# A two-layer decoder trunk: the mixing of the expert rows moves from VectorE to ScalarE and GpSimd

## The reference

```python
top_v, top_i = lax.top_k(h @ w_router, 2)
top_w = jax.nn.softmax(top_v, axis=-1)
# gates: top_w at the two experts of each token, 0 elsewhere
for e in range(N_EXPERTS):
    out = out + gates[:, e:e + 1] * ((silu(h @ w_gate[e]) * (h @ w_up[e])) @ w_down[e])
x = x + g2 * out
return rmsnorm(x, final_g)
```

## Time and profile before

| | us |
|---|---|
| median of 3 runs (lowest, highest) | 1311.26 (1309.56, 1312.83) |
| time of the profiled execution | 1308.28 |
| its span, first to last instruction | 1306.5 |
| TensorE (PE) busy | 1240.5 |
| VectorE (DVE) busy | 1082.4 |
| ScalarE (ACT) busy | 818.2 |
| GpSimd (POOL) busy | 52.3 |
| last turn, about | 1192 to 1294 |

### The profile page before, as it was taken

One profiled execution on the slowest core, in us unless ns is written; L12 is line 12 of the kernel. 1 busy time (PEld: TensorE's weight loads), 2 busy tenths in 40 slices (PEclk: granted clock), 3 DMA queues, 4 the chain that ended last, 5 costly groups with the idle time before them and its releaser, 6 DMA issues.

```text
span 1306.5 us, 17451 instructions
## 1 busy us (share of the span) xinstructions
PE 1240.5 (95%) x5431; PEld 869.8 (67%) x5431; DVE 1082.4 (83%) x1389; ACT 818.2 (63%) x1169; POOL 52.3 (4%) x71
## 2 busy tenths in 40 slices
PE   5999979999989988999999999999999999999996
PEld 1445757777767766666676676676676776776664
DVE  2858877888779766988988988998988988898896
ACT  3125534444445654777777777777777777777774
POOL 2101000000000101000000000000000000000000
PEclk8999989999999998999999999999999999999999
DMA  9996838888867435999999999999999999999991
GB/s 294 388 387 228 277 112 317 295 278 297 315 216 265 162 109 198 303 365 364 363 365 366 365 366 365 363 368 366 361 370 366 354 371 366 360 372 369 372 369 57
DMA packets 277871, 409.61 MB, mean 314 GB/s; under 512 B 6676, under 2 KB 209436, under 8 KB 277572
## 3 DMA queue, kind: packets, MB, share of 16 engines
q1 hardware_dynamic: 273732, 393.82, 87.8%
q0 software_dynamic: 4096, 15.25, 3.6%
HBM read 401.70 MB, written 7.34 MB: 313 GB/s over the span
## 4 chain that ended last, share of the span: by engine, by line
PE 78%; DVE 8%; SPq 7%; issue 3%; ACT 2%; DMA 2%; DVEq 0%; POOL 0%; ACTq 0%; POOLq 0%
PE bank L1814 22%; PE bank L1815 22%; PE bank L1816 22%; PE bank L1964 5%; SPq L607 5%; DVE w_lo L1195 2%; PE bank L1842 1%; ACT w_hi L773 1%; DMA raw<-in_w_ada 1%; DVE more_lo L1195 1%; SPq L591 1%; DMA raw<-in_moe_w_up 1%; PE bank L2269 1%; DVE ada_acc L1247 1%; PE bank L1849 1%
## 5 line engine op out<-in xcount | busy, mean ns | idle before, releaser
L1195 DVE TENSOR_TENSOR w_lo<-raw,w_hi 128x1024 fp32r<-128x1024 f32 x366 | 445.0, 1221 | 78.2 <-ACT w_hi L773 75.5
L773 ACT ACTIVATE w_hi<-raw 128x1024 fp32r<-128x1024 f32 x366 | 381.9, 1052 | 86.7 <-PE bank L1816 80.7
L1195 DVE TENSOR_TENSOR more_lo<-raw,more_hi 128x1024 fp32r<-128x1024 f32 x264 | 308.1, 1218 | 2.5 <-ACT more_hi L773 2.5
L773 ACT ACTIVATE more_hi<-raw 128x1024 fp32r<-128x1024 f32 x264 | 260.4, 1048 | 0.0
L1814 PE MATMUL bank<-more_hi,hgT_hi 128*96 128x512 f32 x368 | 149.8, 407 | 2.1 <-DVE more_lo L1195 2.1
L1814 PE MATMUL bank<-w_hi,hT_hi 128*128 128x512 f32 x320 | 136.7, 427 | 15.6 <-DVE hT_lo L1282 8.6
L1815 PE MATMUL bank<-more_hi,hgT_lo 128*96 128x512 f32 x368 | 144.9, 394 | 0.0
L1816 PE MATMUL bank<-more_lo,hgT_hi 128*96 128x512 f32 x368 | 144.7, 393 | 0.0
L1247 DVE SCALAR_TENSOR_TENSOR ada_acc<-raw,silu_c,ada_acc 128x512 f32<-128x512 f32 x152 | 114.7, 755 | 22.6 <-DMA raw<-in_w_ada 15.8
L1814 PE MATMUL bank<-w_hi,hgT_hi 128*96 128x512 f32 x336 | 132.6, 395 | 0.0
L1815 PE MATMUL bank<-w_hi,hgT_lo 128*96 128x512 f32 x336 | 132.6, 395 | 0.0
(11 more groups left out here) (280 smaller groups left out, 1696.0 us busy)
## 6 DMA issues: line engine op xcount, KB each, us to landing
raw<-in_moe_w_gate SPq DMA_DIRECT2D x88, 1024.0 KB, 11.3
raw<-in_moe_w_up SPq DMA_DIRECT2D x88, 1024.0 KB, 13.6
raw<-in_moe_w_down SPq DMA_DIRECT2D x88, 1024.0 KB, 11.9
raw<-in_w_ada SPq DMA_DIRECT2D x48, 1024.0 KB, 10.6
raw<-in_w_in SPq DMA_DIRECT2D x20, 1024.0 KB, 14.2
raw<-in_ffn_w_gate SPq DMA_DIRECT2D x11, 1024.0 KB, 5.5
raw<-in_ffn_w_up SPq DMA_DIRECT2D x11, 1024.0 KB, 8.0
raw<-in_ffn_w_down SPq DMA_DIRECT2D x11, 1024.0 KB, 11.0
```

Of the source, the lines that this page charges most:

```text
L773: act.activation(like(hi_of(s)), src, ACT.Copy).then_inc(hi_done, 1)
L1195: dve.tensor_tensor(like(lo_of(s)), src, like(hi_of(s).bitcast(F32)), ALU.subtract).then_inc(split_done, 1)
```

## The change

ScalarE scales both rows of each token, each with its own weight: eight scalings instead of four, four in block 5 and four in block 6. The remaining three steps of a quarter become two additions and a product on GpSimd, behind the loading of the pairs, in the same order of quarters; GpSimd waits for the two scalings of the quarter and, between its own steps, for the step before. VectorE's quarters in blocks 6 to 9 are gone; its wait for the twelve steps at the end stays. What is computed is the same.

```diff
-        first_half = sem("first_half")
+        pair_scaled = sem("pair_scaled")
...
@@ gpsimd, behind the loading of y_pairs
+            def mix_quarter(n):
+
+                a, half = BY_TILE[n]
+                cols = slice(CB * half, CB * half + CB)
+                both = y_pairs[a][:, 0, cols]
+                xs = x[:, a, cols]
+                pool.wait_ge(pair_scaled, 2 * n + 2)
+                pool.tensor_tensor(both, both, y_pairs[a][:, 1, cols], ALU.add).then_inc(mix_done, 1)
+                pool.wait_ge(mix_done, 3 * n + 1)
+                pool.tensor_tensor(both, both, mod[:, G2, cols], ALU.mult).then_inc(mix_done, 1)
+                pool.wait_ge(mix_done, 3 * n + 2)
+                pool.tensor_tensor(xs, xs, both, ALU.add).then_inc(mix_done, 1)
+
+            for n in range(4):
+                mix_quarter(n)
@@ scalar, blocks 5 and 6 of the last turn
                         for half in range(2):
                             cols = slice(CB * half, CB * half + CB)
-                            act.activation(y_pairs[a][:, 0, cols], y_pairs[a][:, 0, cols], ACT.Copy,
-                                           scale=w12[:, a, 0:1]).then_inc(first_half, 1)
+                            for c in range(2):
+                                act.activation(y_pairs[a][:, c, cols], y_pairs[a][:, c, cols], ACT.Copy,
+                                               scale=w12[:, a, c:c + 1]).then_inc(pair_scaled, 1)
@@ vector, the last turn
-                        if last and b in (6, 7, 8, 9) and q == 2:
-                            mix_quarter(b - 6)
...
-                dve.wait_ge(first_half, n + 1)
-                dve.scalar_tensor_tensor(out=both, in0=y_pairs[a][:, 1, cols], scalar=w12[:, a, 1:2], in1=both,
-                                         op0=ALU.mult, op1=ALU.add).then_inc(mix_done, 1)
-                dve.wait_ge(mix_done, 3 * n + 1)
-                dve.tensor_tensor(both, both, mod[:, G2, cols], ALU.mult).then_inc(mix_done, 1)
-                dve.wait_ge(mix_done, 3 * n + 2)
-                dve.tensor_tensor(xs, xs, both, ALU.add).then_inc(mix_done, 1)
```

## The result

The changed kernel takes 1315.83 us in the median of 20 runs (1312.21 to 1320.02), against 1311.45 us (1308.83 to 1314.38) for the kernel before. The ratio is 1.0037, with a 95% interval of 1.0027 to 1.0047: **slower by 3.5 to 6.2 us**, 4.9 in the middle.

What follows compares the result with a forecast made beforehand. VectorE was taken to set the pace from 1240.4 to 1278.7 us, TensorE afterwards. Alternating turns move block 8's down pass from 1278.73 to 1283.4: 4.7 us slower, 1311.26 + 4.7 = 1316.0 us, range 1309.8 to 1318.8.

Steps and rivals of the forecast that it cites:

- The gain on VectorE: Last turn: VectorE loses four mixing quarters of 2.11 us; with nothing in their place, 4.5 us gained.
- ScalarE's price: Block 5: two more scalings delay the down-projection splits and TensorE's pass by 1.3 us; block 6's not counted again.
- The turns: GpSimd instructions reading SBUF and VectorE's two-SBUF-input splits exclude each other: held turns of 1.13 and 1.07 us, 2.20 a pair.
- the ten pairs: GpSimd's last ten instructions alternate with ten VectorE splits, blocks 4 to 7, at 2.20 us each, ending at 1261.4.
- the third of block 7: VectorE's third split of block 7, ending at 1262.5 instead of 1253.77; the fourth starts 6.6 us later.
- The splits might not be held: Rival: VectorE and GpSimd work side by side, splits stay at 1.22 us; -3.2 us, 1308.1; chance 0.08.
- VectorE keeps the port: Rival: GpSimd gets in only at a block's two bank-reading VectorE instructions; -1.4 us, 1309.9; chance 0.10.
- The clock: Rival: TensorE's clock falls during waits before block 4's and 5's down passes; +4.7 to +7.5 us, middle 1317.4; chance 0.10.
- the main case: Last turn: GpSimd's instructions and VectorE's splits alternate; 4.7 us slower, 1316.0 us; chance 0.70.
- GpSimd, taken alone: Twelve instructions at 1.3 us are 15 us from 1236.2, done 40 us before VectorE waits for them; by length alone hidden.

Runs made afterwards that it cites:

- the first two experiments: Changed kernel without GpSimd's twelve instructions: ratio 0.9976 to the kernel before; the same with ScalarE's scalings left out too: 0.9960.
- the kernel with two instructions a block: Changed kernel with GpSimd's twelve instructions spread by waits, two a block from block 5 to 10: ratio 1.0012 to the kernel before.
- the filled waits: Changed kernel with ten idle TensorE matmuls ahead of the wait for the hidden half in blocks 5 and 6: ratio 1.0029 to the kernel before.

## Why the prediction was right

**The gain on VectorE** was right in size. The prediction had at most 4.5 us to be had in the last turn; without any mixing it was 5.0 us by the trace (74.7 to 69.7) and 5.2 by the runs, in a kernel that has lost ScalarE's four scalings of before as well.

**ScalarE's price** was right to 0.3 us: 1.3 us forecast for the two more scalings in block 5 where nothing else holds VectorE. The 1.4 us between the first two experiments are for all eight; the waits give 1.0 (TensorE) to 1.2 us (VectorE) for the ones added. That the ones of block 6 would not count again came true: with all eight and no GpSimd arithmetic TensorE's pass behind them does not wait.

**The turns** were the term that decided, and were right in kind and size: 1.13 us for a GpSimd turn and 1.07 for a split's. A held split that follows another takes 2.29 us, start to start 2.2, which is the sum. Ten held splits were forecast in the ten pairs, and the third of block 7 behind the last; eleven came. GpSimd's last instruction ended 0.15 us from its forecast.

**"The splits might not be held"** and **"VectorE keeps the port"** fell as explanations of this change: alternation held from 1242.9 to 1265.1 us without a gap. The second is not wrong everywhere, as the kernel with two instructions a block shows.

**The clock** was a rival with a chance of 0.10, and in the profiled execution it came about, on top of the main case: 1.1 us between two passes, as the filled waits show. The chance was too low. The waits that I had worked out (3.4 us; 3.21 and 3.15 were measured) were longer than any in that turn before (1.21 us), and the one fall that the prediction shows lies right behind a stretch in which TensorE was mostly idle. Its cost was within the 1.4 us stated for one fall, and less than the 13 matmuls at 0.43 us instead of 0.23 would make (2.6 us), since most of the rest is time that TensorE loses to VectorE anyway: with the waits filled and the clock up, pass to pass is 10.10 us, 1.6 above its own 8.5, with waits of 0.39 and 0.72 us in it.

By the trace the sum is 4.7 (turns and scalings) + 1.1 (clock) = 5.8 against 5.7 measured. By the runs it is 4.9, and the interval of 3.5 to 6.2 holds the case without the fall and the one with it. The granted clocks point to the one with it in most runs. So the mechanism was right in its main part and left out a part that came too, and that the forecast of 1316.0 lies 0.2 us from the median is in part luck.

**A slip without effect.** By the prediction's own numbers GpSimd, taken alone, is done about 45 us before VectorE waits for it (1236.2 + 15 against 1296.8), not 40.

## What to carry to other kernels

Before moving elementwise work from VectorE to GpSimd, look at what VectorE does at that time: if its instructions have two SBUF inputs, GpSimd's additions and products that read SBUF don't run beside them but between them, and 1.13 us on GpSimd takes 1.07 us from VectorE, where the same step done by VectorE itself takes 0.7. When an engine sets the pace for a few blocks only, first look for its idle time before and behind: the same twelve steps, one a block and six in the tail, gained 4.2 us where the move to another engine lost 4.9. And a scaling that is "free" on an unsaturated engine still delays what stands behind it in its queue.

## What the runs showed of the hardware that was not expected

- Two GpSimd instructions each waited 3.98 us and missed a turn that others at the same kind of place got (split, `mT_lo`, split). Both had started 0.21 us before a VectorE split did, while another was running; one that started 0.33 us before a split (1251.53) got its turn. What decides it was not tried, and stays open.
- A fill by GpSimd of 128x1024 (0.95 us) runs beside two-input splits without delay on either side.
- TensorE's clock fell behind a single wait of 3.28 us and behind one of 2.56 us in a turn where it was dense before and after. In the changed kernel it stayed up behind the first wait, of 3.21 us, and fell with the second, of 3.15; so the length of a wait alone doesn't decide it, and what does stays open. With ten idle matmuls in the wait it didn't fall.
